# Two exponentials in another order: ScalarE's queue in the first layer's scan products

## The chip, the cores and the metric

One core of a Trainium2 chip runs the whole program, a two-part network, in one launch. The metric is the device time of one execution in microseconds (us); three runs are given and their median is the kernel's time. Everything on the engines' rows below comes from one profiled execution. The engines are TensorE (PE, with its weight loads PEld), VectorE (DVE), ScalarE (ACT), GpSimd (POOL) and SyncE (SP, which here issues DMAs). Each runs its own list of instructions in order, and they meet at semaphores.

## The reference, cut to what matters

The first block has a state space scan over chunks of 128 tokens, in two directions (the second on flipped inputs). With 16 heads and 512 tokens, the part that this case is about is, for each head and direction:

```
a_cum = jnp.cumsum(a, axis=-1)                       # a = dt * a_head
l_intra = jnp.exp(segsum(a))                         # exp(a_cum[t] - a_cum[s]), s <= t, else 0
y_diag = jnp.einsum('bclgn,bcsgn,bgrcls,bcsgrp->bclgrp', cc, bc, l_intra, xdt)
...
y_off = jnp.einsum('bclgn,bcgrpn,bgrcl->bclgrp', cc, prev_states, jnp.exp(a_cum))
y = (y_diag + y_off)
```

Two exponentials are needed for each: that of the cumulated sums, which scales the queries `cc`, and that of their differences, which weighs the products of `cc` and `bc` within a chunk.

## The kernel before

The kernel is written engine by engine: `prod_t`, `prod_a`, `prod_v` and `prod_g` are the lists of TensorE, ScalarE, VectorE and GpSimd for this stage, and `S.on(...)` and `S.at(...)` are the named semaphore counts that tie them together. The stage runs over 16 heads `h`, in eight pairs `o`; a piece `n = 2h + d` is one direction `d` of one head, over all 512 tokens. Every four heads (a group `g`) TensorE multiplies the group's B and C ("cb", line 1102), and VectorE masks the result for both directions ("cbm", line 1178).

For one piece `n`:

1. TensorE spreads the piece's cumulated sums over 128 partitions, into one of four PSUM banks ("sums", line 1116). From n = 4 on it waits until the bank's former user is read ("decay" and "decay min" of n - 4).
2. ScalarE takes the exponential of the bank into one of four SBUF pieces ("decay", line 1152). It waits for "sums" n, and from n = 4 on for the products that last read that piece.
3. VectorE subtracts each token's own sum from the same bank and cuts at zero, in four instructions of 128 columns ("decay min", line 1189). It waits for "decay" n first.
4. ScalarE takes the exponential of these differences in place ("decay exp", line 1154).
5. GpSimd multiplies the first exponential with C ("queries", line 1224). The second exponential is multiplied with the masked product of B and C ("weights"): by GpSimd for even n (line 1228), by VectorE for odd n (line 1194).
6. TensorE does the head's 32 small matmuls ("products", lines 1137 and 1138) once queries and weights of both its pieces are there.

TensorE's list is written out by hand: the sums of head h (both pieces), then the products of head h - 1, then the sums of head h + 1, then the products of head h. On VectorE the addition into the output (line 1213) follows the weights of every even head from the third on. ScalarE's list goes through the pieces one after another, with both exponentials of a piece side by side. Behind the stage ScalarE, VectorE and GpSimd split the input of the next projection (lines 290 and 293), and TensorE goes on with that projection (lines 274 to 276).

Of the kernel before, what the change touches and what calls it, by code (L numbers as in the profile page):

```python
# [9 lines left out]
ACT = mybir.ActivationFunctionType  # L10
# [96 lines left out]
class Program:  # L107
# [1033 lines left out]
    def prod_a(self, a):  # L1141
        S, L, PS = self.S, self.L1, self.PS
        self.after(a, "a", "states")
        self.weights_a(a, 32)
        a.activation(self.stat(4)[:, 0:1], self.cst("one1"), ACT.Exp).then_inc(*S.on("a"))
        for o in range(8):
            for n in range(4 * o, 4 * o + 4):
                ea, dm = self.v(L.WK + 512 * (n % 4), 512), self.v(L.WK + 2048 + 512 * (n % 4), 512)
                a.wait_ge(*S.at("sums", n))
                if n >= 4:  # L1150
                    a.wait_ge(*S.at("products", n // 2 - 2))
                a.activation(ea, PS[self.SUMS[n % 4]][:, :], ACT.Exp).then_inc(*S.on("a", "decay", n))
                a.wait_ge(*S.at("decay min", n))
                a.activation(dm, dm, ACT.Exp).then_inc(*S.on("a", "decay exp", n))
        a.wait_ge(*S.at("cb", 3))
        for k in range(8):
            a.wait_ge(*S.at("xn back", k))
            if k == 6:
                a.wait_ge(*S.at("queries", 31))
            self.part_hi(a, self.v(L.XR[k], 512), L.XN2 + 512 * k, 512, "xn hi", k)  # L1160
# [3634 lines left out]
```

## Time and profile before

| | before |
|---|---|
| time, three runs | 4295.59, 4309.15, 4316.83 us; median 4309.15 |
| the profiled execution | 4287.66 us, span 4285.6 us |
| PE busy | 4078.0 us (95%) |
| DVE busy | 3054.3 us (71%) |
| ACT busy | 1809.0 us (42%) |
| POOL busy | 1531.6 us (36%) |
| line 1152, first exponential | 32 times 580 ns, from 248.6 to 336.9 us |
| line 1154, second exponential | 32 times 630 ns, from 250.8 to 338.7 us |

The stage runs from about 248 to 344 us of the span. In the rows further down, a line of the timeline has the start in us, the duration in us (from the first start to the last end where several instructions are merged), engine, line, operation, output and input, the number of instructions, and in brackets how long the engine was idle before it and what released it. Tile names are coarse: nearly all SBUF data is `A`, all PSUM is `ps`.

### The profile page before, as it was taken

To read this page: it belongs to the slowest core of one execution; us is meant where nothing else is said; L and a number is where in the kernel's file an instruction comes from. 1 tells how busy PE (TensorE), PEld (TensorE's weight loads), DVE (VectorE), ACT (ScalarE), POOL (GpSimd) and SP (SyncE) were. 2 spreads that over 40 slices of the span, in tenths; PEclk is the share of its full clock that TensorE was granted. 3 is DMA by queue.
4 is the path that set the end of the run, shared out by engine and by line. 5 is a ranking of instruction groups with operands and counts; after the bars stand their busy time and mean duration, and the time that the engine had idled before them with its cause. 6 is when DMAs were issued, how large, how long until landed. Compare 5 with 4: busy or idle time off the path is not lost.

```text
span 4285.6 us, 66623 instructions
## 1 busy us (share of the span) xinstructions
PE 4078.0 (95%) x26203; PEld 3554.8 (83%) x26203; DVE 3054.3 (71%) x5007; ACT 1809.0 (42%) x2851; POOL 1531.6 (36%) x1025
## 2 busy tenths in 40 slices
PE   7989998999999999999999999999999999999998
PEld 5767744879999999999899867799889877877997
DVE  5876679458878978888798356598388445656973
ACT  4346432234345643333355255455255333324552
POOL 2054201127998867888512100212111110112121
PEclk9999998999999999999999999999999999999999
DMA  5123521325989999999733321233233232002332
GB/s 192 64 94 122 184 71 40 115 84 194 315 308 341 392 377 369 388 383 375 252 99 98 100 76 64 69 99 104 89 99 106 96 107 89 27 37 71 112 99 74
DMA packets 237550, 683.03 MB, mean 159 GB/s; under 512 B 23399, under 2 KB 85751, under 8 KB 235192
## 3 DMA queue, kind: packets, MB, share of 16 engines
q1 hardware_dynamic: 110528, 389.87, 26.7%
q0 software_dynamic: 47968, 176.48, 10.9%
q10 hardware_dynamic: 78744, 112.43, 7.5%
q8 instruction: 209, 3.42, 0.3%
q14 instruction: 101, 0.83, 0.1%
HBM read 617.21 MB, written 61.44 MB: 158 GB/s over the span
## 4 chain that ended last, share of the span: by engine, by line
PE 53%; DVE 12%; DMA 8%; issue 4%; POOL 3%; ACT 2%; ACTq 1%; DVEq 0%; POOLq 0%
PE ps L274 9%; PE ps L276 8%; PE ps L275 8%; PE ps L2912 5%; PE ps L2913 5%; PE ps L2914 5%; DMA A<-in_u_rows,A 4%; DMA A<-acts 2%; DMA A<-in_v_rows,A 2%; DVE A L2160 2%; PE ps L3947 2%; DVE A L2173 1%; POOL r L243 1%; ACT r L237 1%; DVE r L243 1%
## 5 line engine op out<-in xcount | busy, mean ns | idle before, releaser
L274 PE MATMUL ps<-r,r 128*128 128x352 f32 (+1 forms) x3944 | 1419.9, 360 | 43.3 <-DVE r L243 27.4
L276 PE MATMUL ps<-r,r 128*128 128x352 f32 (+1 forms) x3944 | 1402.0, 355 | 0.0
L275 PE MATMUL ps<-r,r 128*128 128x352 f32 (+1 forms) x3944 | 1400.5, 355 | 0.0
L237 ACT ACTIVATE r<-A 128x1024 fp32r<-128x1024 f32 x513 | 540.0, 1054 | 1027.2 <-PE ps L276 814.6
L243 DVE TENSOR_TENSOR r<-A,r 128x1024 fp32r<-128x1024 f32 x390 | 524.4, 1347 | 615.2 <-ACT r L237 614.9
L274 PEld LDWEIGHTS ps<-r,r 128*128 128x128 f32 x3944 | 745.9, 189 | 140.9 <-DVE r L243 29.0
L275 PEld LDWEIGHTS ps<-r,r 128*128 128x128 f32 x3944 | 746.1, 189 | 78.6 <-issue 3.6
L276 PEld LDWEIGHTS ps<-r,r 128*128 128x128 f32 x3944 | 745.6, 189 | 76.0
L290 ACT ACTIVATE r<-A 128x512 fp32r<-128x512 f32 (+1 forms) x796 | 470.7, 607 | 577.1 <-DVE A L2592 318.5
L2912 PE MATMUL ps<-r,r 128*128 128x256 f32 x2128 | 595.5, 280 | 3.5 <-DVE A L3076 2.5
L2914 PE MATMUL ps<-r,r 128*128 128x256 f32 x2128 | 594.4, 279 | 0.0
L2913 PE MATMUL ps<-r,r 128*128 128x256 f32 x2128 | 594.3, 279 | 0.0
L293 POOL TENSOR_TENSOR r<-A,r 128x352 fp32r<-128x352 f32 (+2 forms) x243 | 336.8, 1393 | 693.0 <-ACT r L290 570.3
L293 DVE TENSOR_TENSOR r<-A,r 128x512 fp32r<-128x512 f32 x617 | 454.1, 752 | 9.1 <-ACT r L290 5.3
L2912 PEld LDWEIGHTS ps<-r,r 128*128 128x128 f32 x2128 | 403.4, 190 | 5.4 <-DVE A L3076 3.4
L2914 PEld LDWEIGHTS ps<-r,r 128*128 128x128 f32 x2128 | 403.4, 190 | 0.0
L2913 PEld LDWEIGHTS ps<-r,r 128*128 128x128 f32 x2128 | 403.2, 189 | 0.2
L3094 POOL TENSOR_TENSOR A<-A 128x512 f32<-128x512 f32 x72 | 121.2, 1683 | 677.5 <-DVE A L3085 677.5
L243 POOL TENSOR_TENSOR r<-A,r 128x1024 fp32r<-128x1024 f32 x123 | 308.9, 2512 | 111.7 <-ACT r L237 110.2
L2144 POOL DMA_INDIRECT A<-in_v_rows,A x160 | 253.5, 1584 | 30.9 <-issue 14.3
L2173 DVE SCALAR_TENSOR_TENSOR A<-A 128x1024 f32<-128x1024 f32 x158 | 216.6, 1371 | 21.8 <-DMA A<-in_v_rows,A 18.4
L3164 DVE TENSOR_TENSOR A<-A 128x512 f32<-128x512 f32 x304 | 208.6, 686 | 4.5 <-issue 1.6
(561 smaller groups left out, 5364.5 us busy)
## 6 DMA issues: line engine op xcount, KB each, us to landing
A<-in_pu SPq DMA_DIRECT2D x128, 512.0 KB, 5.0
A<-in_pv SPq DMA_DIRECT2D x128, 512.0 KB, 7.0
A<-in_f1i SPq DMA_DIRECT2D x88, 512.0 KB, 3.5
A<-in_f2i SPq DMA_DIRECT2D x88, 512.0 KB, 3.4
A<-in_w_in SPq DMA_DIRECT2D x48, 512.0 KB, 3.7
gates<-A ACTq DMA_DIRECT2D x8, 2816.0 KB, 13.5
A<-gates ACTq DMA_DIRECT2D x32, 704.0 KB, 10.9
A<-in_f1o SPq DMA_DIRECT2D x44, 512.0 KB, 3.5
```

What stands on the lines that cost most here:

```text
L237: a.activation(self.vr(self.wr0 + 2048 * (u % RW), 1024), self.v(self.st0 + 1024 * (u % RS), 1024), ACT.Copy).then_inc(*self.S.on("a", "hi ...
L243: e.tensor_tensor(self.vr(at + 1024, 1024), self.v(self.st0 + 1024 * (u % RS), 1024), self.vr(at, 1024).bitcast(F32), ALU.subtract).then_i ...
L274: t.matmul(o, hi, xh, start=first and k == k0, stop=False)
L275: t.matmul(o, hi, xl, start=False, stop=False)
L276: m = t.matmul(o, lo, xh, start=False, stop=final and k == K - 1)
L290: a.activation(self.vr(at, n), src, ACT.Copy).then_inc(*self.S.on("a", *key))
L293: e.tensor_tensor(self.vr(lo, n), src, self.vr(at, n).bitcast(F32), ALU.subtract).then_inc(*self.S.on(who, *key))
L2144: g.indirect_dma_start(self.v(L.ROWS + 1024 * (n % 6), 1024), None, self.T["u_rows" if n < NG else "v_rows"], bass.IndirectOffsetOnAxis(in ...
L2173: v.scalar_tensor_tensor(out=acc, in0=row, scalar=w, in1=acc, op0=ALU.mult, op1=ALU.add).then_inc(*S.on("v", "row used", n))
L2912: t.matmul(ps[:, 0:256], hi, xh, start=opens and k == 0, stop=False, skip_group_check=not opens)
L2913: t.matmul(ps[:, 0:256], hi, xl, start=False, stop=False, skip_group_check=not opens)
L2914: m = t.matmul(ps[:, 0:256], lo, xh, start=False, stop=k == 3, skip_group_check=not opens)
```

## The change

ScalarE's list in `prod_a` is put in another order. The first exponential of piece n now stands ahead of the second exponential of piece n - 1; the first of all comes alone, and the second exponential of piece 31 comes alone at the end. The waits stay with their instructions. No other engine's list is changed.

```diff
-        for o in range(8):
-            for n in range(4 * o, 4 * o + 4):
-                ea, dm = self.v(L.WK + 512 * (n % 4), 512), self.v(L.WK + 2048 + 512 * (n % 4), 512)
+        for n in range(33):
+            if n < 32:
                 a.wait_ge(*S.at("sums", n))
                 if n >= 4:
                     a.wait_ge(*S.at("products", n // 2 - 2))
-                a.activation(ea, PS[self.SUMS[n % 4]][:, :], ACT.Exp).then_inc(*S.on("a", "decay", n))
-                a.wait_ge(*S.at("decay min", n))
-                a.activation(dm, dm, ACT.Exp).then_inc(*S.on("a", "decay exp", n))
+                a.activation(self.v(L.WK + 512 * (n % 4), 512), PS[self.SUMS[n % 4]][:, :], ACT.Exp).then_inc(*S.on("a", "decay", n))
+            if n:
+                dm = self.v(L.WK + 2048 + 512 * ((n - 1) % 4), 512)
+                a.wait_ge(*S.at("decay min", n - 1))
+                a.activation(dm, dm, ACT.Exp).then_inc(*S.on("a", "decay exp", n - 1))
```

## Rows read from the trace of the kernel before

**Rows 1.** Table by stage: us, PE, PEld, DVE, ACT, POOL, PEclk, DMA share, GB/s.

```profile
262.00:345.00 83.00, 73.28 (x563) 59.66 (x562) 53.12 (x143) 36.71 (x64) 54.00 (x43) 1.00 0.08 27
```

**Rows 2.** Waits from 250 to 345 us: waiter <- releaser, total us, times, longest us.

```profile
DVE A L1189 <- ACT A L1152: 20.4, 17, 1.5
PE ps L1137 <- DVE A L1194: 13.7, 12, 4.1
...
ACT A L1152 <- PE ps L1116: 10.2, 10, 3.1
```

**Rows 3.** Timeline of TensorE, 316 to 328 us.

```profile
316.26 1.16 PE L1102 MATMUL ps<-A 128*128 128x128 f32 x8
317.35 1.13 PE L1116 MATMUL ps<-A 32*128 32x512 f32 x4
322.04 1.13 PE L1116 MATMUL ps<-A 32*128 32x512 f32 x4
324.27 0.40 PE L1137 MATMUL ps<-A 128*64 128x128 f32 x2 [1.10 <-DVE A L1194]
...
327.88 1.13 PE L1116 MATMUL ps<-A 32*128 32x512 f32 x4
```

**Rows 4.** Timeline of ScalarE, 322 to 330 us.

```profile
322.62 0.63 ACT L1154 ACTIVATE A<-A 128x512 f32<-128x512 f32 x1 [1.19 <-DVE A L1189]
...
325.85 0.63 ACT L1154 ACTIVATE A<-A 128x512 f32<-128x512 f32 x1 [2.06 <-DVE A L1189]
326.39 0.58 ACT L1152 ACTIVATE A<-ps 128x512 f32<-128x512 f32 x1
328.16 0.63 ACT L1154 ACTIVATE A<-A 128x512 f32<-128x512 f32 x1 [1.19 <-DVE A L1189]
329.04 0.60 ACT L1152 ACTIVATE A<-ps 128x512 f32<-128x512 f32 x1 [0.24 <-PE ps L1116]
```

**Rows 5.** Timeline of VectorE, 317 to 330 us.

```profile
317.97 1.28 DVE L1178 TENSOR_TENSOR A<-ps,A 128x512 f32<-128x512 f32 x2
...
323.28 0.84 DVE L1194 TENSOR_TENSOR A<-A 128x512 f32<-128x512 f32 x1 [0.70 <-ACT A L1154]
324.05 0.74 DVE L1213 SCALAR_TENSOR_TENSOR A<-A,ps 128x512 f32<-128x512 f32 x1
...
327.00 1.13 DVE L1189 TENSOR_SCALAR A<-ps,A 128x128 f32<-128x128 f32 x4 [1.18 <-ACT A L1152]
328.82 0.84 DVE L1194 TENSOR_TENSOR A<-A 128x512 f32<-128x512 f32 x1 [0.70 <-ACT A L1154]
```

**Rows 6.** Timeline of all engines at the stage's start, 252 to 262 us.

```profile
252.78 1.27 POOL L1224 TENSOR_TENSOR A<-A 128x512 f32<-128x512 f32 x1
...
253.75 0.84 DVE L1194 TENSOR_TENSOR A<-A 128x512 f32<-128x512 f32 x1 [0.69 <-ACT A L1154]
...
261.11 1.13 PE L1116 MATMUL ps<-A 32*128 32x512 f32 x4
```

**Rows 7.** Timeline of all engines at the stage's end, 333 to 344 us.

```profile
333.42 1.13 PE L1116 MATMUL ps<-A 32*128 32x512 f32 x4
333.80 0.84 DVE L1194 TENSOR_TENSOR A<-A 128x512 f32<-128x512 f32 x1 [0.70 <-ACT A L1154]
...
338.36 1.27 POOL L1224 TENSOR_TENSOR A<-A 128x512 f32<-128x512 f32 x1
...
340.33 0.40 PE L1137 MATMUL ps<-A 128*64 128x128 f32 x2 [1.87 <-DVE A L1194]
...
343.94 0.50 PE L274 MATMUL ps<-r,r 128*128 128x512 f32 x1
```

**Rows 8.** Timeline of TensorE in a later stage, 543 to 555 us.

```profile
543.56 1.99 PE L1580 MATMUL ps<-A 64*128 64x512 f32 x8
548.16 3.47 PE L1580 MATMUL ps<-A 64*128 64x512 f32 x8 [2.62 <-DVE A L1616]
553.79 1.13 PE L1649 MATMUL ps<-A 128*128 128x512 f32 x2 [2.16 <-DVE A L1623]
```

## The prediction

> **What bounds the kernel now.** TensorE is busy 95% of the span on the page, but the change lives in one stretch of some 92 us, so the shares of the whole say little and I read that stretch alone. First the table by stage [rows 1]: from 262 to 345 us TensorE is busy 73.3 of 83 us at a granted clock of 1.00, VectorE 53.1, ScalarE 36.7, GpSimd 54.0. No engine is full, so this stage is set by waits between engines, in a loop over 16 heads. In what follows h is a head, n = 2h or 2h+1 a piece (one direction of one head); D(n) is the exponential of the sums from PSUM (line 1152), M(n) VectorE's four subtractions (1189), E(n) the exponential of the differences (1154), W(n) the weights (1194 on VectorE for odd n, 1228 on GpSimd for even n), Q(n) the queries (1224), S(h) TensorE's start on the sums of both pieces of head h (1116), P(h) its start on that head's 32 products (1137 and 1138).
>
> Second the waits of the stretch [rows 2]. TensorE's products wait 13.7 us for W on VectorE. VectorE's M waits 20.4 us for D, nearly always 1.18 us: it stands idle while ScalarE finishes E(n) and then does D(n+1), whose sums had long been there. That is what the edit can take away. But D itself waits 10.2 us in 10 places for TensorE's sums. That is the row that decides, because it says the sums of the next head are not early.
>
> Third, one turn of the loop, engine by engine. TensorE's order is S(h+1), P(h), S(h+2), P(h+1): the sums of a head stand behind the products of the head before the last. The starts are S(12) 317.35, S(13) 322.04, P(12) 324.27, S(14) 327.88 [rows 3]. ScalarE goes E(25) 322.62, (D(26) between), E(26) 325.85, D(27) 326.39, E(27) 328.16, D(28) 329.04 [rows 4]. VectorE does W(25) 323.28, M(27) 327.00, W(27) 328.82 [rows 5]. Note E(27) at 328.16: it starts *before* D(28) at 329.04, and W(27) at 328.82 has begun before the sums of head 14 can be used at all. So P(13) overlaps with waiting for those sums. The mean turn is (333.42 - 261.11) / 13 = 5.56 us from S(2) to S(15) [rows 6, 7], the four groups' extra matmuls included.
>
> **The change part by part.** No instruction is added or taken away: 32 D and 32 E remain, no DMA, no queue of SP or GpSimd is touched. Only the order on ScalarE is new: D(n+1) stands ahead of E(n).
>
> *The odd piece of the same head (D(2h+1) ahead of E(2h)), 16 times.* Its sums are ready: S(13) has both pieces at 322.04 + 1.13 [rows 3], D(27) ran only at 326.39 [rows 4]. This takes away the idle 1.18 us before M(2h+1) [rows 5], at no cost, since ScalarE was idle for about 2.06 us before E(26) [rows 4]. Left alone it would be worth up to 1.18 us a head.
>
> *The first piece of the next head (D(2h+2) ahead of E(2h+1)), 15 times.* Here the new wait stands in front of what TensorE needs. D(2h+2) waits for S(h+1), which TensorE issues only after P(h-1) is through. Queued behind D(2h+2) on ScalarE is E(2h+1); VectorE's W(2h+1) waits for that; P(h) waits for W(2h+1); and S(h+2) stands behind P(h). It isn't a deadlock, since S(h+1) precedes P(h), but it closes a serial ring with no overlap:
>
> - P(12) to S(14): 327.88 - 324.27 = 3.61 us [rows 3]
> - S(14) to D(28), ScalarE idle and waiting for it: 329.04 - 327.88 = 1.16 us [rows 3, 4].
> - D to the E behind it. The trace has no such pair. The nearest is the other way round: D(27) follows E(26) at 0.54 us though E lasts 0.63, an overlap of 0.09 [rows 4]; D lasts 0.60, so I take 0.50. Bounds 0.48 and 0.60 (no overlap).
> - E(27) to W(27): 328.82 - 328.16 = 0.66 us [rows 4, 5]
> - W(25) to P(12): 324.27 - 323.28 = 0.99 us [rows 3, 5]
>
> Sum: 3.61 + 1.16 + 0.50 + 0.66 + 0.99 = 6.92 us a head. Everything else has room in it. After W(2h-1), which starts 0.99 us before P(h-1), VectorE has the output addition (0.74) every second head, M(2h) and M(2h+1) (1.13 each) and in three heads the masks (1.28) [rows 5], so it is through some 3 us after P(h-1), when E(2h+1) can't start before 3.61 + 1.16 + 0.50 = 5.27. GpSimd's three multiplications (1.27 each, one of them in [rows 7]) end near 5.7 of 6.92 even then. So the 1.18 us won in M are hidden: the odd piece's gain is worth nothing.
>
> *The group matmuls (line 1102)* stand ahead of S(4), S(8), S(12). Their 317.35 - 316.26 = 1.09 us [rows 3] lay partly in slack; in the ring they count fully, three times: 3.3 us.
>
> *Start of the loop.* P(0) waited for W(1), which ended at 253.75 + 0.84 = 254.59 [rows 6]. M(1) is now earlier by up to 1.18 us, but Q(1) on GpSimd ended at 252.78 + 1.27 = 254.05 [rows 6] and isn't moved, so P(0) gains at most 0.54 us; I take 0.3 to S(2), with 0 and 0.54 as bounds.
>
> *From S(2) to S(15)*: before 72.3 us [rows 6, 7]. After, 13 turns: 13 x 6.92 + 3.3 = 93.2 us. Difference 20.9 us.
>
> *Last head.* There is no D(32), so E(31) is free of the ring. W(29) came 333.80 - 333.42 = 0.38 us after S(15) before; now 1.16 + 0.50 + 0.66 = 2.32. From W(29) on runs an unchanged chain over M(30), E(30), W(30) to Q(31): 338.36 - 333.80 = 4.56 us. Q(31) lasts 1.27, and P(15) follows 0.15 to 0.67 us after (the trace doesn't show one that GpSimd alone released): S(15) + 8.3 to 8.8, instead of 340.33 - 333.42 = 6.91 [rows 7]. That adds 1.4 to 1.9, I take 1.65.
>
> *Behind the stage* the projection's matmuls start at 343.94, right behind the last products [rows 7]. They follow P(15) whatever its time, and DMA is idle there (share 0.08, [rows 1]), with the loads of the stretch long landed; so I see nothing that swallows the delay.
>
> Sum: 20.9 + 1.65 - 0.3 = +22.3 us. With the bounds of the D to E step (13 x -0.02 to +0.10) and of the ends it is +21.5 to +24. The profiled execution took 4287.66 us (span 4285.6), and would take 4310; it was 21.5 us quicker than the median of the runs, 4309.15, so for the median I add the same: 4331.5 us.
>
> **The rivals.**
>
> *A. The clock falls (slower still).* In the ring TensorE works 3.61 + 1.13 us and then is idle for 6.92 - 4.74 = 2.18 us in each head, where now the idle time before products is 1.1 us or none [rows 3]. The trace shows the clock surviving an idle time of 2.16 us (two matmuls of line 1649 in 1.13 us behind it) and not surviving one of 2.62 us (eight of line 1580 take 3.47 instead of 1.99 us) [rows 8]. My 2.18 lies next to the first, but comes 14 times over. If it fell to 1.2 GHz, the 32 products would take up to 3.6 us more: 14 x 3.6 = 50, in all +73 us, 4382; a few heads of it give 4340 to 4355. The Trainium skill, page "TensorE: Matmul & The Clock Gate", section "A second HAM failure mode: psum-queue depth-cycling", says that frequent short idles between groups of matmuls can make the clock swing between its levels; by that rule this rival is the outcome. The rows of this stage, with idles of 0.2 to 1.9 us and a clock of 1.00 throughout, don't bear it out so far. Chance 0.12.
>
> *B. Faster.* Were D(2h+2) always ready when ScalarE comes to it, E(2h+1) would lose nothing and M would gain 1.18 us a head. The turn would fall from 5.56 towards TensorE's own 3.61 + 1.13 = 4.74, plus 3.3 / 13 = 0.25 for the group matmuls, 0.57 us a head, some 8 us: 4301. It decides at the point where S(h+1) plus 1.16 us comes before M(2h+1) ends. Against it speak the 10 places where D waits for TensorE even in its late position [rows 2]. It would be within 0.5% anyway. Chance 0.03 (with 0.01 for a gain beyond 0.5%).
>
> *C. No change.* The delay is only partly real, because some later stage waits for something that this one doesn't move, or because the ring is looser than I make it: 0 to +10 us, 4309 to 4319. For it speaks only that I haven't followed each later wait; against it the idle DMA queues. Chance 0.08.
>
> **How the numbers follow.** Forecast 0.77, A 0.12, B 0.03, C 0.08. About 0.5% (21.5 us) is what a measurement can tell from no change, and my +22.3 stands on that line; the three runs shown spread over 21 us, so the forecast's own chance splits about evenly, 0.41 over and 0.36 under. Slower: 0.41 + 0.12 = 0.53. Faster by over 0.5%: 0.01, with the scatter of the runs 0.02. Same: 0.45. Range: the forecast's +20 to +25 with a scatter of some 12 us on a median gives 4318 to 4346; reaching to C below and to the mild end of A above, 4310 to 4352.
>
> **What would show it.** Right: in the changed trace E(2h+1) starts 0.5 us behind D(2h+2), and ScalarE's long waits are for TensorE's sums, not VectorE's M; S to S is 6.9 us, 8.0 with the group matmuls; M no longer waits 1.18 us for D(2h+1); products wait some 2.2 us for W each time; the first projection matmul starts near 366 instead of 343.94. Wrong: turns of 5 to 5.6 us (B or C), a granted clock under 1.00 between 262 and 365 us (A), or a first projection matmul that is late while the span isn't (C).

## The result, and the profile after

The changed kernel takes 4367.24 us (median of four runs; 4362.77 to 4370.14), the kernel before 4303.89 us by four runs, 63 us less. The ratio, estimated from all the runs, is 1.0133 with a 95% interval of 1.011 to 1.0156, so the change is slower by 47 to 67 us; the quotient of the two medians, 1.0147, lies within it. The forecast was slower too, by 22 us. The profiled executions stand further apart, 4370.14 against 4287.66 us, since that of before was the fastest seen of it. Where they part can be followed by the first start of the same lines: 58.6 us at the projection behind the stage, 61.8 us at 740 us, 71.4 at 2163 and 82.5 at the end. Only the first 58.6 lie in the stage that was changed, and they alone match the runs; the rest is scattered over stages in which nothing was changed. I take it for the spread of single executions, which no run shows as such.

The table by stage for the same stretch as [rows 1], and the waits from 250 to 390 us, beside [rows 2] (in the new file the exponentials are lines 1151 and 1155, the differences 1190, the odd weights 1195, the queries 1225, the even weights 1229):

```profile
262.00:345.00 83.00, 59.02 (x323) 50.24 (x320) 35.77 (x90) 20.08 (x36) 32.78 (x27) 0.77 0.08 26
```

```profile
DVE A L1195 <- ACT A L1155: 76.7, 14, 7.3
ACT A L1151 <- PE ps L1116: 67.4, 14, 6.5
...
PE ps L1137 <- DVE A L1195: 32.0, 12, 2.7
...
DVE A L1190 <- ACT A L1151: 0.6, 1, 0.6
```

In 83 us TensorE now gets through 323 matmuls instead of 563, and its granted clock is 0.77 instead of 1.00 (1.00 being 2.4 GHz). The wait that the edit was to remove is gone (VectorE's differences wait 0.6 us for the first exponential, where it was 20.4). In its place stand 67.4 us of ScalarE waiting for TensorE's sums, and 76.7 us of VectorE's weights waiting for the second exponential behind it.

One turn of the loop, beside [rows 3], [rows 4] and [rows 5]; timeline of all engines, most of TensorE's products left out:

```profile
318.68 1.13 PE L1116 MATMUL ps<-A 32*128 32x512 f32 x4
319.84 0.60 ACT L1151 ACTIVATE A<-ps 128x512 f32<-128x512 f32 x1 [6.44 <-PE ps L1116]
320.33 0.62 ACT L1155 ACTIVATE A<-A 128x512 f32<-128x512 f32 x1
320.51 1.27 POOL L1225 TENSOR_TENSOR A<-A 128x512 f32<-128x512 f32 x1 [4.49 <-ACT A L1151]
...
320.99 1.34 DVE L1195 TENSOR_TENSOR A<-A 128x512 f32<-128x512 f32 x1 [7.22 <-ACT A L1155]
...
322.47 0.40 PE L1137 MATMUL ps<-A 128*64 128x128 f32 x2 [2.67 <-DVE A L1195]
322.71 0.38 PE L1138 MATMUL ps<-A 128*64 128x128 f32 x2
...
323.85 0.63 PE L1137 MATMUL ps<-A 128*64 128x128 f32 x2
...
327.75 1.13 PE L1116 MATMUL ps<-A 32*128 32x512 f32 x4
328.90 0.60 ACT L1151 ACTIVATE A<-ps 128x512 f32<-128x512 f32 x1 [3.68 <-PE ps L1116]
...
331.54 0.66 PE L1137 MATMUL ps<-A 128*64 128x128 f32 x2 [2.67 <-DVE A L1195]
...
338.01 1.13 PE L1116 MATMUL ps<-A 32*128 32x512 f32 x4
```

The ring is there as forecast: sums, first exponential 1.16 us later, second exponential 0.49 behind it, weights 0.66 behind that, products, sums. Two things in it are not as forecast. The weights last 1.34 us instead of 0.84, so that products start 3.79 us behind the sums instead of 3.31, and TensorE's idle time is 2.67 us instead of 2.18. And the products take 327.75 - 322.47 = 5.28 us, then 338.01 - 331.54 = 6.47, where full clock gives 3.61. The clock shows in the rows of two products each: at full clock such a row lasts 0.38 us, and from 323.85 on 0.63. From 331.5 to 337.4 us the granted clock is 0.50, which is 1.2 GHz. It falls now within the products, as here, now in the idle time ahead of them, as before those at 331.54. In 12 of the 13 turns from the sums of head 2 to those of head 15 they are slow. These 13 turns take 127.5 us, against 72.3 before and 93.2 forecast.

At the end of the stage, beside [rows 7]:

```profile
389.20 1.13 PE L1116 MATMUL ps<-A 32*128 32x512 f32 x4
...
402.57 0.50 PE L274 MATMUL ps<-r,r 128*128 128x512 f32 x1
```

### The profile page after: what moved, and what is told of

Its sections match the earlier page's. It is cut to its first block, busy times and chain, and to the rows that moved or that the text cites. A ratio compares the mean times of both kernels' runs of the same rounds, so it can differ in the third digit from the quotient of the medians.

```text
span 4368.0 us, 66623 instructions
## 1 busy us (share of the span) xinstructions
PE 4118.6 (94%) x26203; PEld 3593.4 (82%) x26203; DVE 3063.9 (70%) x5007; ACT 1808.1 (41%) x2851; POOL 1536.4 (35%) x1025
## 4 chain that ended last, share of the span: by engine, by line
PE 52%; DVE 12%; DMA 7%; issue 4%; POOL 3%; ACT 2%; ACTq 1%; DVEq 0%; POOLq 0%
PE ps L274 8%; PE ps L276 8%; PE ps L275 8%; PE ps L2913 5%; PE ps L2914 5%; PE ps L2915 5%; DMA A<-in_u_rows,A 3%; DMA A<-acts 2%; DMA A<-in_v_rows,A 2%; POOL r L243 2%; PE ps L3948 2%; DVE A L2161 2%; DVE A L2174 1%; ACT r L237 1%; POOL A L2145 1%
```

## The experiments

S(2) to S(15) below means the time from the start of the sums of head 2 to that of head 15, read in the profiled execution: 72.3 us before, 127.5 in the changed kernel. "Slow products" are those of the 13 turns between, from the first of a head to the next head's sums or group matmuls, that take 5.1 us or more. The time is the median, each set against the runs of the kernel before on its own chip; the ratio is estimated from all runs, and lies within 0.2% of the quotient of the medians. "The whole stage" is the time from the first sums of all to the projection, 99.5 us before and 158.1 in the changed kernel. S(2) to S(15), the whole stage and the slow products are read from one execution of each kernel. In the expectations D(n), E(n), S(h), P(h) have the prediction's meaning.

### The two halves of the edit

Within a head alone, ScalarE's order is D(2h), D(2h+1), E(2h), E(2h+1):

```diff
-        for o in range(8):
-            for n in range(4 * o, 4 * o + 4):
...
+        for kind, n in [(k, 2 * h + d) for h in range(16) for k in "DE" for d in range(2)]:
```

> Only the half of the edit within a head: ScalarE does D(2h), D(2h+1), E(2h), E(2h+1), and E(2h+1) never stands behind the next head's sums. Theory (the loss comes wholly from D(2h+2) ahead of E(2h+1), which closes a ring over TensorE): the ring is open, M(2h+1) starts right behind M(2h), a turn from sums to sums falls from 5.56 us to about 5.0 (TensorE's own 3.61 + 1.13 and a quarter of 1.09), the clock stays at 1.00, the stage ends 6 to 9 us earlier than before: about 4296 where the kernel before takes 4304. Rival (any look-ahead on ScalarE delays the second exponential and with it the weights): slower than before by 5 us or more.

Measured: 4309.66 us against 4313.99, ratio 0.9994 (0.9979 to 1.0008), no difference. S(2) to S(15) 71.1 us, a turn of 5.47 instead of 5.56; no slow products but at the start. The theory's direction holds (no loss without the step across heads, and the rival's 5 us of loss is not there), but its gain isn't there either: the whole stage took 100.0 us, against 99.5. The timeline shows what took its place:

```profile
326.34 1.13 PE L1116 MATMUL ps<-A 32*128 32x512 f32 x4
326.29 0.89 DVE L1195 TENSOR_TENSOR A<-A 128x512 f32<-128x512 f32 x1 [0.70 <-ACT A L1155]
326.59 2.94 POOL L1225 TENSOR_TENSOR A<-A 128x512 f32<-128x512 f32 x2
328.56 0.40 PE L1137 MATMUL ps<-A 128*64 128x128 f32 x2 [1.10 <-DVE A L1190]
```

VectorE's weights were through at 327.18, yet the products start at 328.56, with the end of GpSimd's first query multiplication of the two; it stands behind the even weights and lasts 1.7 us beside VectorE's. The row names the differences as releaser; those queries are the only other thing that the products wait for.

Across heads alone, D(2h+2) ahead of E(2h+1), E(2h) ahead of D(2h+1):

```diff
+        for kind, n in [("D", 0)] + [x for h in range(16) for x in (("E", 2 * h), ("D", 2 * h + 1)) + ((("D", 2 * h + 2),) if h < 15 else ()) + (("E", 2 * h + 1),)]:
```

> Only the other half: D(2h+2) ahead of E(2h+1), but E(2h) ahead of D(2h+1) as before. Theory: the whole loss is here; turns of 9 to 10 us as in the changed kernel, the last sums near 389 us, +55 to +65 us on the time. Rival (the pair within a head has a share in the loss): clearly less, under +45 us.

Measured: 4371.34 us against 4313.99, ratio 1.015 (1.0123 to 1.0176), +57 us; S(2) to S(15) 127.8 us and the whole stage 158.1 us, as in the changed kernel. The whole loss lies in the step across heads.

### What the two multiplications do to each other

GpSimd's queries of the next head wait until VectorE's weights are through:

```diff
                 g.wait_ge(*S.at("decay", n))
+                if n % 2 == 0 and n:
+                    g.wait_ge(*S.at("weights", n - 1))
```

> The changed kernel, with GpSimd's queries of the next head's first piece waiting for VectorE's weights of the odd piece, so that the two don't run side by side. Theory (the weights take 1.34 instead of 0.84 us because both engines multiply at once, and that 0.5 us lifts TensorE's idle time from 2.18 to 2.66 us, past the 2.62 at which the clock was seen to fall): weights 0.84 us, idle 2.18 us, clock 1.00, turns of 6.92 us (8.0 with the group matmuls), +22 us on the time. Rival (the clock falls with repeated idle times of 2.2 us as well): weights 0.84, but products of 5 to 6.5 us in half of the heads, +40 to +50 us.

Measured: 4337.44 us against 4313.99, ratio 1.0056 (1.0034 to 1.0077), +23 us. S(2) to S(15) 94.4 us, the whole stage 123.4 us. The same turn, all engines:

```profile
316.62 1.13 PE L1116 MATMUL ps<-A 32*128 32x512 f32 x4
317.77 0.60 ACT L1151 ACTIVATE A<-ps 128x512 f32<-128x512 f32 x1 [3.68 <-PE ps L1116]
318.27 0.62 ACT L1155 ACTIVATE A<-A 128x512 f32<-128x512 f32 x1
...
318.92 0.69 DVE L1195 TENSOR_TENSOR A<-A 128x512 f32<-128x512 f32 x1 [4.46 <-ACT A L1155]
...
319.76 1.27 POOL L1227 TENSOR_TENSOR A<-A 128x512 f32<-128x512 f32 x1 [3.04 <-DVE A L1195]
```

Alone, the weights last 0.69 us, not even 0.84: the 0.84 of before had some overlap in it too (GpSimd's like multiplication ended at 322.31 + 1.26 = 323.57, the weights that started at 323.28 at 324.12, again 0.55 later). The products start 3.14 us behind the sums, a turn at full clock is 6.75 us, and TensorE's idle time is 2.02 us. Eleven products of 13 are at full clock; two took 5.28. So the one added wait on GpSimd takes away 33 us of the 55, most of them by way of the clock.

### The clock by itself

Two matmuls that nobody reads fill TensorE's idle time in the changed kernel:

```diff
+                if h == 3:
+                    t.wait_ge(*S.at("modset", 7))
+                if h >= 3:
+                    for _ in range(2):
+                        t.matmul(PS[6][:, :], self.cst("ident"), self.v(L.ACT, 512), start=True, stop=True)
                 if h:
                     self.products_t(t, h - 1)
```

> The changed kernel, with two more matmuls (identity by the sums' rows, 128 by 512, into a bank that nobody reads) behind each head's sums from head 3 to 15, to keep TensorE busy in the idle time of 2.66 us. Theory (about 28 us of the loss is the clock, the rest the ring): clock 1.00 from head 3 on, products 3.6 us in each head, turns of 7.4 us as by 3.61 + 1.16 + 0.49 + 0.65 + 1.34 + 0.15, or up to 0.3 more if the added matmuls last longer than the idle time; the stage ends some 25 us earlier than in the changed kernel, +32 to +38 us on the time. Rival (products are slow for another reason than the idle time, such as the weights' contention): products stay at 5 to 6.5 us in half of the heads and the time stays at +60 or rises.

Measured: 4340.22 us against 4313.99, ratio 1.0064 (1.0039 to 1.009), +26 us, less than the 32 to 38 expected; the whole stage took 131.0 us, +31.5, which lies in the interval. More work for TensorE, and the changed kernel loses about half as much. From head 3 on every turn is the same:

```profile
317.02 1.13 PE L1116 MATMUL ps<-A 32*128 32x512 f32 x4
320.81 0.40 PE L1142 MATMUL ps<-A 128*64 128x128 f32 x2 [0.75 <-DVE A L1200]
324.42 1.13 PE L1116 MATMUL ps<-A 32*128 32x512 f32 x4
328.21 0.40 PE L1142 MATMUL ps<-A 128*64 128x128 f32 x2 [0.75 <-DVE A L1200]
```

The products still start 3.79 us behind the sums, so the ring with its 1.34 us weights is untouched, and they take 3.61 us: turns of 7.40. S(2) to S(15) is 101.2 us, which is 13 x 7.40 + 3 x 1.09 + 1.66 for the one slow head ahead of the filling. The rest up to 127.5, 26.3 us, is the clock.

Both remedies together (the wait on GpSimd, and one such matmul instead of two):

> The changed kernel with both remedies: GpSimd's queries wait for VectorE's weights (no multiplications side by side), and one matmul of 128 by 512 behind each head's sums from head 3 on (TensorE's idle time about 1.07 us). Theory (three terms that add up: the ring, +18.7 us between the sums of head 2 and 15; the multiplications side by side, +8.5; the clock, +28): every turn from head 3 on is 6.75 us (7.84 with the group matmuls), sums 2 to 15 take 91 to 93 us, where they took 94.4 with the first remedy alone and 101.2 with the second alone; +20 us on the time. Rival (the terms hang on each other): turns other than 6.75 us.

Measured: S(2) to S(15) 92.7 us, every turn from head 3 on 6.75 us (and 7.84 with the group matmuls), as forecast by the sum of terms. The time was 4336.54 us against 4305.27, ratio 1.0078 (1.0053 to 1.0103), +31 us, which is more than the 20 expected; from the first sums to the projection the stage took 122.1 us, 22.6 more than the 99.5 of before, so the other 8 or so are not in the stage. The profiled execution was the fastest of the five, 4329.08 us; where the rest of the median lies isn't shown.

### How much idle time the clock stands

The same kernel with one smaller matmul in the idle time, of 128 columns:

```diff
+                    for _ in range(1):
+                        t.matmul(PS[6][:, 0:128], self.cst("ident"), self.v(L.ACT, 128), start=True, stop=True)
```

> The changed kernel with one small matmul (128 by 128) behind each head's sums from head 3 on, so that TensorE's idle time is about 2.4 us, between the 2.02 at which the clock held in every head and the 2.66 at which it fell in about half. If the clock's fall depends on the idle time alone with a limit near 2.6: clock 1.00, turns of 7.4 us, +33 us. If it depends on how the work lies over a longer stretch: a fall in some of the heads, between one in eight and one in three, +38 to +50 us.

and with 160 and 224 columns:

> The changed kernel with one matmul of 128 by 160 behind each head's sums from head 3 on. By the run with 128 columns (idle 2.25 us) and that with 2 x 512 (idle 0.76), an idle time of about 2.19 us, which is the one that the prediction had put down as safe, on one matmul pair behind 2.16 us in the kernel before. If the limit is that row: clock 1.00, turns 7.40 us, +33 us. If repeated idle times count for more than a single one: falls in some heads as with 2.25 us, +40 to +50 us.

> The same with 128 by 224, an idle time of about 2.06 us, beside the 2.02 at which the clock held in the run without side by side multiplications. If the idle time decides: clock 1.00, turns 7.40 us, +33 us. If the share of busy time in a turn matters as well (here 5.3 of 7.4 us, there 4.7 of 6.75): the clock holds as well, and more surely. If it falls here, neither is the whole rule.

| kernel | idle before products, us | turn at full clock, us | slow products of 13 | S(2) to S(15), us | time against before |
|---|---|---|---|---|---|
| changed | 2.67 | 7.40 | 12 | 127.5 | 1.0133 (1.011 to 1.0156) |
| 128 columns | 2.25 | 7.40 | 13 | 130.7 | 1.0113 (1.0095 to 1.0131) |
| 160 columns | 2.20 | 7.40 | 10 | 120.8 | 1.0085 (1.0055 to 1.0114) |
| 224 columns | 2.09 | 7.40 | 7 | 111.1 | 1.0092 (1.0058 to 1.0127) |
| weights apart | 2.02 | 6.75 | 2 | 94.4 | 1.0056 (1.0034 to 1.0077) |
| both remedies | 0.96 | 6.75 | 1, ahead of the filling | 92.7 | 1.0078 (1.0053 to 1.0103) |
| 2 x 512 columns | 0.75 | 7.40 | 1, ahead of the filling | 101.2 | 1.0064 (1.0039 to 1.009) |

In all filled kernels the first products of the 13, P(1), have the unfilled idle time before them; they are slow in each of these kernels, and count. With 224 columns every second head is slow, by 1.66 us, in step; TensorE's timeline:

```profile
327.93 0.40 PE L1142 MATMUL ps<-A 128*64 128x128 f32 x2 [2.09 <-DVE A L1200]
331.54 1.13 PE L1116 MATMUL ps<-A 32*128 32x512 f32 x4
...
335.33 0.40 PE L1142 MATMUL ps<-A 128*64 128x128 f32 x2 [2.09 <-DVE A L1200]
340.61 1.13 PE L1116 MATMUL ps<-A 32*128 32x512 f32 x4
```

Neither branch of my expectations holds whole. There is no limit at 2.6 us, nor at 2.16: idle times of 2.09 us already cost, and with the weights apart even 2.02 did, twice. The number of slow heads falls with the idle time, but between 2.09 with 7 and 2.02 with 2 the turn is different too, so these two can't be set down to the idle time alone. The medians don't order as the profiled S(2) to S(15) do; with 160 columns the runs went from 4341 to 4379 us and the profiled one was the slowest, as it was with 128 columns. In the profiled executions the whole stage is 61, 53 and 43 us longer than before with 128, 160 and 224 columns, where the medians are 48, 31 and 39 us longer. So how often the clock falls probably varies from one execution to the next, and the counts of the table, from one execution each, can be too high for the usual one. With 160 columns two of the five runs were only 24 and 25 us above the median of before, no more than the kernel without slow products behind the filling (+26).

### Where the ring closes

TensorE's sums one place earlier in the changed kernel, S(h+2) ahead of P(h):

```diff
-                if h:
-                    self.products_t(t, h - 1)
+                if h > 1:
+                    self.products_t(t, h - 2)
+        self.products_t(t, 14)
         self.products_t(t, 15)
```

> The changed kernel, with S(h+2) ahead of P(h) on TensorE, so that D(2h+2) never waits for sums that stand behind the products. Theory (the ring then closes over the buffer only: D(2h+4) waits for products h): products to D about 3.8, D to E 0.49, E to weights 0.65, weights 1.34 + 0.15, a turn of 6.4 us instead of 7.4 by the same sum, TensorE's longest idle time 1.7 us, clock 1.00, +12 to +16 us on the time against the kernel before. Rival (the sums' place on TensorE was the only link of the ring): turns of 5.6 us or less, no loss against the kernel before.

Measured: 4326.29 us against 4302.92, ratio 1.0054 (1.0036 to 1.0073), +23 us, outside my 12 to 16 though on the theory's side. From P(1) at 268.74 to P(14) at 357.68 a turn is 6.84 us on average; a turn without slow products takes 5.9 to 6.8 us, with up to 2.03 us idle (once 2.73), and three heads had products of over 5 us, which I had not counted on. So taking the sums out of the way opens the ring only in part: the first exponential still waits for the products that free its buffer. ScalarE's wait is now for them, in the waits from 262 to 340 us:

```profile
...
ACT A L1152 <- PE ps L1139: 27.7, 11, 7.8
```

### A version with the gain

The first half alone, and GpSimd does both queries of a head before the even weights:

```diff
-            for n in range(4 * o, 4 * o + 4):
...
+            for h in (2 * o, 2 * o + 1):
+                for n in (2 * h, 2 * h + 1):
+                    ea = self.v(L.WK + 512 * (n % 4), 512)
+                    g.wait_ge(*S.at("decay", n))
+                    g.tensor_tensor(ea, ea, self.v(L.CHC + 512 * q, 512), ALU.mult).then_inc(*S.on("g", "queries", n))
+                n = 2 * h
+                dm = self.v(L.WK + 2048 + 512 * (n % 4), 512)
+                g.wait_ge(*S.at("cbm", q))
+                g.wait_ge(*S.at("decay exp", n))
+                g.tensor_tensor(dm, dm, self.v(L.WKB + 1024 * (q % 2), 512), ALU.mult).then_inc(*S.on("g", "weights", n))
```

> As the run with only the half within a head (D(2h), D(2h+1), E(2h), E(2h+1)), and GpSimd does both queries of a head first, then the weights of the even piece. Theory (in that run the gain was small because in every second head TensorE's products waited 1.10 us for GpSimd's queries of the odd piece, which stood behind its weights of the even piece): that wait falls to some 0.3 us or goes, the mean turn goes from 5.47 to about 5.0 us, 6 us less than in that run, 8 to 10 us less than before: about 4302 where the kernel before takes 4312. Rival (GpSimd has 3 multiplications of 1.27 to 1.7 us in each head and is full whatever their order; the weights of the even piece are then as late as the queries were): the turn stays at 5.4 to 5.5.

and with TensorE's sums one place earlier as well:

> The same, and TensorE issues the sums of a head one place earlier: S(h+2) ahead of P(h). Theory (with ScalarE's pairs the turn is set by TensorE's own 3.61 + 1.13 and 1.09 every fourth head, so 5.0): no further change beyond 2 us, as D still waits for the products that free its buffer. Rival (ScalarE's idle time before D, for the sums, is on the path): another 0.3 us a head or more, 4 us.

Measured: 4300.6 us against 4302.92, ratio 0.9993 (0.9972 to 1.0013), and 4299.42 us, ratio 0.9993 (0.9978 to 1.0007). In the traces the stage is shorter, from the first sums to the projection 94.3 and 93.4 us against 99.5 before. S(2) to S(15) is 67.1 us in the first, a turn of 5.16, and the wait of 1.10 us in every second head is 0.43. So the mechanism is as forecast, and the gain in the stage is 5 to 6 us, less than the 8 to 10 expected. The sums' earlier place counted for more in the loop than the theory gave it: from P(1) to P(14) the second version took 63.8 us and the first 67.6, as its products up to P(13) don't wait for the weights but stand back to back with the sums; 2.8 of the 3.8 us were lost ahead of P(1). The time of the whole kernel can't tell either gain from nothing. Neither is a version that I could call faster.

## Why the prediction was right or wrong

**What sets the end, right.** The step across heads closes a ring over TensorE. Its half alone gives the whole loss (127.8 against 127.5 us), the other half none, and the steps between sums, first exponential, second exponential and the start of the weights came out at 1.16, 0.49 and 0.66 us, against 1.16, 0.50 and 0.66 forecast. That the 1.18 us won in the differences would be worth nothing is right too: with that half left out the loss is the same.

**The weights' duration, wrong, a term mis-sized by 0.49 us.** The step "W(25) to P(12), 0.99 us" took the duration of weights that ran nearly alone. In the ring the first exponential releases GpSimd's queries 0.67 us after its start and the second releases VectorE's weights 1.15 us after it, so the two always run side by side. In all rows the weights end about 0.55 us behind the end of the queries: in the changed kernel 320.51 + 1.27 = 321.78 and 320.99 + 1.34 = 322.33; in the kernel before, for W(7), these rows show the same 0.55 and were there to be read:

```profile
271.95 1.27 POOL L1224 TENSOR_TENSOR A<-A 128x512 f32<-128x512 f32 x1
...
272.57 1.20 DVE L1194 TENSOR_TENSOR A<-A 128x512 f32<-128x512 f32 x1 [0.70 <-ACT A L1154]
```

The turn is then 3.61 + 3.79 = 7.40 and not 6.92, and 13 turns cost 6.2 us more. The Trainium skill, page "SBUF — State Buffer", section "SBUF: two separate sides", says that a VectorE instruction with two inputs in SBUF and a GpSimd one can't hold the port pair that they share at the same time: the one that starts first has it for its whole instruction, and the other waits. By it the weights would end about their own 0.69 us behind the queries; the rows show 0.55, near it, and that the one that starts second is the one that gets longer. I had not applied it to instructions that the edit brings together.

**The clock, wrong, and by most.** I gave rival A a chance of 0.12 and its mild end +31 to +46 us, on the ground that one idle time of 2.16 us [rows 8] had left the clock alone. That was a single case, and it had no row of repeated idle times of that size beside it. In its place the runs show repeated idle times of 2.67 us, after nearly each of which the clock was down for part or all of the products. The clock fell in 12 of 13 turns and cost 28 us of the 34 that the forecast missed in S(2) to S(15):

| term, S(2) to S(15) | us |
|---|---|
| before | 72.3 |
| ring with weights alone, full clock (13 x 6.75 + 3.3) | +18.7 |
| weights beside the queries (13 x 0.65) | +8.4 |
| clock (the rest up to 127.5) | +28.1 |

The kernel with both remedies confirms the first, that with filling the second, and the removal of either cause nearly takes away the third. Product by product, the time above 3.61 us in the 13 turns adds up to the same 28.1 us. Had my 2.18 us been the true idle time, the clock could still have fallen: with 2.20 us it did in 10 of 13 products of the profiled execution, though other runs of that kernel took as little as if it hadn't, and no run had my turn of 6.92 us. So 2.18 us was no safe value, and the step that failed is the one that took a single surviving idle time for a bound; how much of the clock's 28 us the 0.49 us of longer weights brought about stays open. The Trainium skill, page "TensorE: Matmul & The Clock Gate", section "A second HAM failure mode: psum-queue depth-cycling", says that frequent short idles between groups of matmuls can make the clock swing, which the prediction named and set aside. This trace agrees: the clock fell in 12 of 13 turns.

**The last head and the rest.** S(15) to the projection took 13.37 us against 10.52, +2.9 where I had +1.65. In the kernel with both remedies it took 12.30, +1.8, and in that with filling alone 12.96: so the ring's part was right, the longer weights add 0.7 and the clock 0.4. The start had the wrong sign: S(2) came 0.6 us later than before, where I had 0.3 earlier. I had called Q(1) on GpSimd not moved, but it stands behind the even weights, and these wait for E(0), now behind D(1). It started at 253.35 instead of 252.78, beside VectorE's W(1) at 253.32, and lasted 1.79 us instead of 1.27. 55.2 + 2.9 and 0.6 at the start are the 58.6 us of the stage, within rounding. That nothing behind the stage swallows the delay is right. The range ended at 4352 and the time was 4367.24.

## What to carry to other kernels

Before an instruction is put ahead of another on an in-order engine, ask whether what it waits for stands, on some other engine, behind the work that the second one releases. If so, the pipeline becomes a ring, and every short wait in it counts in full. Then price the ring's idle time on TensorE twice, once as time and once as a fall of the clock, and take the durations of instructions from rows in which the same neighbours run beside them.

## What the runs showed of the hardware

- A VectorE multiplication of 128 x 512 with both inputs in SBUF lasts 0.69 us alone, and 1.34 us when a like one on GpSimd (1.27 us) started 0.48 us before it. It ends 0.55 us behind the other. Where VectorE's starts first, GpSimd's gets longer: 1.72 and 1.79 us.
- TensorE's clock can fall again and again where each turn has one idle time of 2.1 to 2.7 us; at 2.02 us it fell twice in 13 turns. 32 products then took 5.1 to 6.5 us instead of 3.61, at a granted clock of 0.50 while it was down. Extra matmuls that nobody reads, cutting that time to 0.75 us, bought back 26 us in this stage. What the chip counts was not settled by these runs.
- On ScalarE, an exponential of 128 x 512 from SBUF starts 0.49 us behind one from PSUM that lasts 0.60, as the opposite order's 0.09 us of overlap had let expect.
